# Two-block transformer forward pass: in forgetting attention, ScalarE and VectorE part the queries and keys of head pairs 2 to 7 in place of GpSimd; in dilated attention VectorE's low part comes one triple later

## The reference, cut to what matters

```python
def banded_attention(q, k, v, n_back):          # dilated attention, 12 heads
    s = jnp.einsum('nbqhd,nbkhd->nbhqk', qb, kc).astype(jnp.float32) * (D ** -0.5)
    s = jnp.where(mask[None, :, None], s, NEG)
    m = jnp.max(s, axis=-1, keepdims=True)
    p = jnp.exp(s - m)
    l = jnp.sum(p, axis=-1, keepdims=True)
    o = jnp.einsum('nbhqk,nbkhd->nbqhd', (p / l).astype(v.dtype), vc)

def fox_mixer(xn, w_q, w_o, k, v, c):           # forgetting attention, 16 heads
    for i in range(T // BLK):                   # blocks of 128 queries
        s = jnp.einsum('bqhd,bkhd->bhqk', q[:, q0:q1], k[:, :q1]).astype(jnp.float32) * scale
        s = s + (c_t[:, :, q0:q1, None] - c_t[:, :, None, :q1])
        s = jnp.where(causal, s, NEG)
        p = jax.nn.softmax(s, axis=-1).astype(v.dtype)
        outs.append(jnp.einsum('bhqk,bkhd->bqhd', p, v[:, :q1]))
```

## Time and profile before

| | |
|---|---|
| median of 3 runs | 3070.67 us (3064.64 to 3075.9) |
| the profiled execution | 3066.08 us |
| its span in the profile | 3064.4 us, 1.7 us shorter than its time |
| mean granted clock of TensorE | 0.984 of full speed |
| dilated attention | about 1905 to 1970 us |
| forgetting attention | about 2527 to 2645 us |

### The profile page before, as it was taken

The page is one execution under the profiler, slowest core; times in us unless marked ns, Lnnn a source line. Parts: engine busy times, 40 slices in busy tenths (PEclk is TensorE's granted clock), DMA queues, the critical chain, the costliest instruction groups (busy, mean ns, idle before and its releaser), DMA issues. The chain is left out here.

```text
span 3064.4 us, 38613 instructions
## 1 busy us (share of the span) xinstructions
PE 2907.5 (95%) x15514; PEld 2375.2 (78%) x15514; DVE 1776.6 (58%) x1996; ACT 1436.1 (47%) x1913; POOL 530.2 (17%) x626
## 2 busy tenths in 40 slices
PE   8999999898999989999999799999999998899998
PEld 4878888786887577777777478788888896688887
DVE  4448755546554778888888264555544316455543
ACT  4345525437213478888788132543333325443332
POOL 0016513224101533223222100000000002000000
PEclk9999999999999999999999999999999998999999
DMA  5220111111752589999999552123322301223331
GB/s 207 56 64 1 41 51 56 28 56 54 228 192 89 201 316 367 363 366 377 376 382 363 219 200 86 56 84 96 110 97 83 105 24 56 76 84 96 96 101 51
DMA packets 278385, 456.07 MB, mean 149 GB/s; under 512 B 24864, under 2 KB 206752, under 8 KB 258112
## 3 DMA queue, kind: packets, MB, share of 16 engines
q1 hardware_dynamic: 251712, 398.82, 36.8%
q0 software_dynamic: 26496, 54.79, 5.0%
HBM read 451.16 MB, written 39.08 MB: 160 GB/s over the span
## 5 line engine op out<-in xcount | busy, mean ns | idle before, releaser
L269 DVE TENSOR_TENSOR weight_part<-weights,weight_part 128x2048 fp32r<-128x2048 f32 (+1 forms) x62 | 140.6, 2267 | 155.8 <-ACT weight_part L258 155.8
L1198 ACT ACTIVATE up_conv<-banks,tap_columns 128x512 f32<-128x512 f32 x88 | 68.7, 781 | 288.3 <-PE banks L316 287.0
L258 ACT ACTIVATE weight_part<-weights 128x2048 fp32r<-128x2048 f32 (+1 forms) x62 | 116.0, 1870 | 170.6 <-PE banks L311 164.4
L786 POOL TENSOR_SCALAR branch_mean<-branch_mean 128x1 f32<-128x1 f32 x20 | 10.7, 537 | 1045.5 <-ACT up_conv L780 704.8
L1242 DVE SCALAR_TENSOR_TENSOR up_conv<-banks,tap_columns,up_conv 128x511 f32<-128x511 f32 x88 | 65.9, 749 | 214.1 <-ACT up_conv L1198 214.1
L311 PE MATMUL banks<-hT_r,weight_part 128*128 128x512 f32 x448 | 175.3, 391 | 0.3 <-PEq L3861 0.3
L316 PE MATMUL banks<-hT_r,weight_part 128*128 128x512 f32 x448 | 174.9, 390 | 0.0
L269 DVE TENSOR_TENSOR weight_part_o<-weights,weight_part_o 128x2048 fp32r<-128x2048 f32 (+2 forms) x46 | 100.0, 2174 | 115.2 <-ACT weight_part_o L258 115.2
L311 PE MATMUL banks<-hT_r,weight_part_o 128*128 128x512 f32 x384 | 149.5, 389 | 0.0
L315 PE MATMUL banks<-h_low,weight_part 128*128 128x512 f32 x384 | 149.4, 389 | 0.0
L315 PE MATMUL banks<-h_low,weight_part_o 128*128 128x512 f32 x384 | 149.4, 389 | 0.0
(11 more groups left out here) (728 smaller groups left out, 8878.6 us busy)
## 6 DMA issues: line engine op xcount, KB each, us to landing
weights<-in_w_e_gate SPq DMA_DIRECT2D x44, 1024.0 KB, 15.6
weights<-in_w_e_up SPq DMA_DIRECT2D x44, 1024.0 KB, 18.4
hT<-in_w_e_down SPq DMA_DIRECT2D x44, 1024.0 KB, 18.8
weights<-in_w_up SPq DMA_DIRECT2D x88, 512.0 KB, 4.7
gate_up<-in_w_e_gate SPq DMA_DIRECT2D x22, 1024.0 KB, 15.8
gate_up<-in_w_e_up SPq DMA_DIRECT2D x22, 1024.0 KB, 18.2
down<-in_w_e_down SPq DMA_DIRECT2D x22, 1024.0 KB, 18.3
weights<-in_w_down SPq DMA_DIRECT2D x20, 1024.0 KB, 4.9
```

Of the source, the lines that this page charges most:

```text
L258: c.nc.scalar.activation(self.pair(n)[0][:, 0:z], self.raw[n % RAW_SLOTS][:, 0:z], ACT.Copy).then_inc(self.high_ready, 1)
L269: c.nc.vector.tensor_tensor(low[:, 0:z], self.raw[n % RAW_SLOTS][:, 0:z], high[:, 0:z].bitcast(F32), ALU.subtract).then_inc(self.low_ready, 1)
L1198: nc.scalar.activation(a[:, f % 2, v], c.ps[:, 2 * (f % 4) + v], ACT.Identity, scale=conv[:, 2, ch:ch + 1], bias=bias[:, ch:ch + 1]).then_ ...
```

## The change: who parts pairs 2 to 7, and when DVE writes a low part

```diff
--- before.py
+++ after.py
@@ -512,7 +512,7 @@
 
         @block.vector
         def _(dve):
-            for i in range(J + 4):
+            for i in range(J + 5):
                 if i < J:
                     z = slice(i % 3, i % 3 + 1)
                     dve.wait_ge(scored, i + 1)
@@ -531,8 +531,8 @@
                     nc.vector.reciprocal(share[:, z], total[:, z]).then_inc(shared, 1)
                     dve.wait_ge(shared, j + 1)
                     nc.vector.tensor_scalar(pr[:, j % 3], pr[:, j % 3], share[:, z], None, ALU.mult).then_inc(scaled, 1)
-                if 0 <= i - 4 < J and (i - 4) % 2:
-                    n = (i - 4) // 2
+                if 0 <= i - 5 < J and (i - 5) % 2:
+                    n = (i - 5) // 2
                     dve.wait_ge(highs, n + 1)
                     nc.vector.tensor_tensor(dst(1, n), drained(n), dst(0, n).bitcast(F32), ALU.subtract).then_inc(lows, 1)
                 if i == J // 2:
@@ -1385,6 +1385,7 @@
         self.chigh = c.over(rows, "cumulated_high", [3 * B_HEADS, SEQ], F32R, D)
         self.tri = c.over(rows, "triangles", [P, 3, P], F32, D + SEQ)
         self.prepared = c.sem("fox_prepared")
+        self.rounded, self.parted = c.sem("fox_rounded"), c.sem("fox_parted")
 
     def more(self, c):
 
@@ -1401,6 +1402,17 @@
         pool.wait_ge(done, 4 * f + 2)
         c.nc.gpsimd.tensor_tensor(kp[:, 1], self.kT[:, f], kp[:, 0].bitcast(F32), ALU.subtract).then_inc(done, 1)
         c.nc.gpsimd.tensor_tensor(qp[:, 1], self.qT[:, f], qp[:, 0].bitcast(F32), ALU.subtract).then_inc(done, 1)
+
+    def high(self, c, act, f, x):
+
+        part, whole = ((self.kp, self.kT), (self.qp, self.qT))[x]
+        c.nc.scalar.activation(part[f % 2][:, 0], whole[:, f], ACT.Copy).then_inc(self.rounded, 1)
+
+    def low(self, c, dve, f, x):
+
+        part, whole = ((self.kp, self.kT), (self.qp, self.qT))[x]
+        dve.wait_ge(self.rounded, 2 * (f - 2) + x + 1)
+        c.nc.vector.tensor_tensor(part[f % 2][:, 1], whole[:, f], part[f % 2][:, 0].bitcast(F32), ALU.subtract).then_inc(self.parted, 1)
 
     def early(self, c):
 
@@ -1441,9 +1453,6 @@
         @block.gpsimd
         def _(pool):
             room.prepare(c, pool, 1)
-            for f in range(2, KD):
-                pool.wait_ge(scored, NT * (f - 1))
-                room.prepare(c, pool, f)
 
         @block.tensor
         def _(pe):
@@ -1451,8 +1460,10 @@
                 if n < U:
                     f, i = divmod(n, NT)
                     W = (i + 1) * P
-                    if i == 0:
+                    if i == 0 and f < 2:
                         pe.wait_ge(room.prepared, 4 * (f + 1))
+                    elif i == 0:
+                        pe.wait_ge(room.parted, 2 * (f - 1))
                     if n >= 2:
                         pe.wait_ge(expd, 2 * (n - 1))
                     for x, (q, k) in enumerate(((0, 0), (0, 1), (1, 0))):
@@ -1507,6 +1518,10 @@
                     f = j // NT
                     act.wait_ge(headed, j + 1)
                     nc.scalar.activation(oT[0][:, f], c.ps[:, 6 + f % 2], ACT.Copy).then_inc(highed, 1)
+                if n < U and n % NT in (0, 1) and 2 <= n // NT + 1 < KD:
+                    if n % NT == 0:
+                        act.wait_ge(scored, n)
+                    room.high(c, act, n // NT + 1, n % NT)
                 if n == U - 1:
                     c.split.high_ahead(c, act)
 
@@ -1532,6 +1547,8 @@
                     f = j // NT
                     dve.wait_ge(highed, f + 1)
                     nc.vector.tensor_tensor(oT[1][:, f], c.ps[:, 6 + f % 2], oT[0][:, f].bitcast(F32), ALU.subtract).then_inc(left, 1)
+                if n < U and n % NT in (1, 2) and 2 <= n // NT + 1 < KD:
+                    room.low(c, dve, n // NT + 1, n % NT - 1)
                 if n == U - 1:
                     c.split.low_ahead(c, dve)
     return oT
```

## The result

The changed kernel takes 3046.51 us, the median of 7 runs (3043.23 to 3052.04), against 3069.93 us for the kernel before, of 7 runs beside it (3060.78 to 3075.9). The ratio is 0.993, with a 95% interval of 0.9917 to 0.9943: 0.7% faster. Its profiled execution took 3045.98 us, with a span of 3044.3 us at a mean granted clock of 0.988 (before: 3066.08, 3064.4 and 0.984).

What follows compares the result with a forecast made beforehand. PE, busy 95% of the span, was taken as the bound. Gains of 17.84 us (windows), 1.3 (dilated attention) and 0 sum to 19.1: 3046.9 from the profiled execution, 3051.5 from the median, middle 3049, range 3042 to 3058 us.

Steps and rivals of the forecast that it cites:

- a floor of 11.17 us: Forgetting attention: six pair windows fall to the length of pair 7's, where POOL rests, a gain of 17.84 us.
- The clock's half: Forgetting attention: the part of the windows' gain that comes from the lowered clock, 9.14 us.
- the clock falling all the same: Rival in forgetting attention: waits go but TensorE still drops to 1.2 GHz in four pairs, 3056.1 us; chance 0.08.
- The costs: Forgetting attention: ACT's twelve copies at 0.60 us and DVE's twelve subtractions at 0.70 fit in idle time, booked at 0.
- Ready about 1.5 us early: Forgetting attention: the queries' low part is done about 1.5 us before PE's next first scores need it.
- slower rival: At each pair's start in forgetting attention, PE waits 2 us for `parted` and the clock falls: 3077.1 us; chance 0.04.
- Dilated attention: Moving DVE's low part shortens PE's waits for ACT's copies in this stage, a gain of 1.3 us.
- The two waits: PE's waits for ACT's copies mid dilated attention: 1.20 us falls to about 0.55, and 0.61 goes.
- the 0.74: Dilated attention: triple 8's masked scores can start up to 0.74 us earlier, of which 0.65 was taken.
- my upper bound of 1.8: Dilated attention: largest gain allowed, with PE's waits of 1.20 and 0.61 us both gone whole.
- The sum: Whole kernel: 17.84 + 1.3 + 0 = 19.1 us off, 3046.9 us from the profiled execution.
- my middle of 3049: Whole kernel: forecast time taken between 3046.9 us from the profiled execution and 3051.5 from the median.

Runs made afterwards that it cites:

- e3: Changed kernel, with POOL doing the same four operations at the same moments on data nobody needs: 3067.6 us, ratio 0.9993.
- e1: Only the forgetting-attention part of the change, dilated attention as in the kernel before: 3052.11 us, ratio 0.9946.
- e6: Changed kernel with the added work doubled, one extra copy or subtraction ahead of each of ACT's twelve and DVE's twelve: 3051.12 us, ratio 0.9938.
- e7: Changed kernel with the parting of the next stage's first weights one round later at forgetting attention's end: 3040.93 us, ratio 0.9917.
- e8: Changed kernel with that later parting at forgetting attention's end, and dilated attention's low part of the weights one round later too: 3046.15 us, ratio 0.9924.
- e9: Changed kernel, with POOL doing only two casts of 128x512 of other data at each of the six moments: 3049.51 us, ratio 0.9937.
- e5: The changed kernel itself once more, unaltered, on another chip: 3052.34 us, ratio 0.9946 to the kernel before.
- e10: Changed kernel, with POOL doing only two subtractions of other data at each of the six moments: 3053.46 us, ratio 0.9953.

## Why the prediction was right

**Where the loss sat.** It was read as six pairs above a floor of 11.17 us, 17.84 us in all; 18.05 went. The small surplus is the first of the windows, at 10.98. That POOL beside DVE is the cause was an inference from two rows, and the kernel with POOL at work for nobody (`e3`) shows it: the same waits, the same windows, and ratio 0.9993. The Trainium skill ("SBUF — State Buffer", section "Who interferes with whom") has whichever of VectorE and GpSimd issues first hold the ports that they share for a whole instruction. The traces agree: 2.77 and 1.76 us for scalings that take 0.75 alone, both more than twice 0.75, the most that equal sharing would give, and each held scaling ends 0.21 or 0.22 us behind the POOL instruction that it met.

**The clock's half.** I booked 9.14 us for it and gave 0.08 to the clock falling all the same. In seven executions without POOL's subtractions and with the parting in its place (the changed kernel twice, `e1`, `e6` to `e9`) all six windows had clock 1.00, so the half is real and goes with the waits. What the Trainium skill describes ("TensorE: Matmul & The Clock Gate", section "A second HAM failure mode: psum-queue depth-cycling"), and I had weighed as a rival, did not come true here: PE still idles 0.13 us in such a window without a fall.

**The costs.** ACT's copy was put at 0.60 and takes 0.63 to 0.64; DVE's subtraction at 0.70 and takes 0.68 to 0.69. Both were booked at nothing, and doubling both left the windows at 11.17. In busy time a pair's two cost less than their rows add up to, 1.20 us for DVE (8.02 in place of my 8.2) and 1.04 for ACT (8.52, not 8.7), since each row starts before the one ahead of it has ended. The cover is about to be used up in one place only, the 0.38 us before ACT's copy of 256 columns.

**The new wait.** "Ready about 1.5 us early" gave the right sign, and the changed kernel has no wait for `parted`. But that slack is no measure of what a later place would cost. One unit later I reckoned with 1.5 to 2 us a pair and it was 3.8, since the subtraction lands behind another that waits itself. My slower rival had this mechanism and priced it too low, at a wait of 2 us and 3077.1 us in place of 3089.93.

**Dilated attention.** 1.3 us were forecast and 1.79 measured, so this term was too small. The two waits that it counts gave 1.14: the second went as said; of the first 0.67 was left where I said 0.55, so 0.12 us more of the 0.74 was lost on the way than I had allowed. What the sum left out are the four delays of some 0.15 us behind other low parts. That the total is my upper bound of 1.8 is chance, since the bound took both waits as gone whole. In the time it can't be seen alone: ratio 0.9998.

**The sum.** From the profiled execution I had 3046.9, and the new one is 3045.98: 0.2 us too little for the windows, 0.5 for dilated attention, 0.2 more from upstream of both. The medians differ by 23.4 us, more than the 19.1 of the sum; on the chip of `e5` they differ by 15.4. That my middle of 3049 came within 2.5 us of the median is therefore partly luck. What moves between such comparisons lies outside both stages: in the trace of `e5` the six windows are the same 66.81 us, but they begin at 2539.46 and not at 2531.66, so 7.8 us had been lost before the stage began. All of it was lost before dilated attention, whose first scores start at 1909.70 and not at 1901.88. It is the same kernel, and its clock is a little lower in `e5` on the way there: 0.98 against 1.00 in the first 100 us and from 400 to 500, 0.95 against 0.98 from 500 to 600. The two places explain 19.8 us; what beyond that a comparison shows is not from the change. Why the clock differs between two runs of one kernel is open.

## What to carry to other kernels

Before work is handed to the engine that seems idle, look at what its neighbour does at that moment: a row that lasts nearly four times its usual length beside another engine's row is a lost resource, though no semaphore names it. Count a wait of a nearly always busy TensorE by the window of the loop and not by the wait alone, because a gap of 1.6 us cost up to 3.0 us more of clock. And when an operation is put in its new place, read what stands ahead of it in that engine's order and what that waits for; a unit's distance says little.

## What the runs showed of the hardware that was not expected

The same gap does not always lower the clock. With a wait of 1.6 us per pair the clock fell in 4 of 6 windows before, in 3 of 6 with dilated attention's part alone, and in 4 of 6 with POOL at work for nobody, each time other ones. With 0.57 us it fell in 0 of 6, with 3.84 us in 6 of 6, each in one execution. A fall costs 1.5 us a pair at a window's mean of 0.88, or 3.0 at 0.78.

POOL's operations held up DVE's scalings, which read and write SBUF; beside DVE's maximum, which reads PSUM, two casts of POOL ran their whole 1.17 us and the maximum took 1.22 us, as it does alone. Beside two subtractions of POOL it took 1.23 us (from 2536.02, in `e10`).

The holding goes the other way too. In another stage of the kernel before, DVE began a subtraction of 128x2048 with both inputs in SBUF at 538.00 (L269, 2.38 us), and a cast of POOL of 128x128 that began at 538.46 lasted 2.07 us (L2718); at 534.17, beside a maximum over PSUM, the same cast took 0.29.
